# A ring of twelve gather slots instead of thirteen, nine kept weight chunks instead of seven, and a gate computed with tanh

## Time and profile before

| | us |
|---|---|
| median of 3 runs | 1592.19 (1591.38 to 1593.02) |
| the profiled execution | 1590.18 |
| its span | 1588.4 |
| PE busy | 1031.0 (65%) |
| DVE busy | 1108.0 (70%) |
| ACT busy | 465.7 (29%) |
| POOL busy | 569.0 (36%) |
| DMA | 646.25 MB, mean 407 GB/s |

### The profile page before, as it was taken

How to read it: one execution, slowest core, us unless ns; L and a number is a source line. 1 busy time by engine, 2 the same in 40 slices (tenths; PEclk the granted TensorE clock), 3 DMA queues, 4 the chain that set the end, 5 groups by cost and what they waited for, 6 DMA issues and landing times.

```text
span 1588.4 us, 20120 instructions
## 1 busy us (share of the span) xinstructions
PE 1031.0 (65%) x6910; PEld 695.9 (44%) x6910; DVE 1108.0 (70%) x3081; ACT 465.7 (29%) x966; POOL 569.0 (36%) x663
## 2 busy tenths in 40 slices
PE   8996877648634477787674478876676444444444
PEld 8995643426401266665452156655363111111111
DVE  3546878675457776986755776997856777777765
ACT  4111563111101335742211334753222111111112
POOL 0013333333223326742322335762332333333330
PEclk9999876868856698888797679987798555555667
DMA  9999999999999999999999999999999999999995
GB/s 368 409 363 388 380 422 421 418 421 418 417 419 422 421 385 416 414 419 418 421 416 419 422 400 377 421 406 419 421 417 415 423 421 421 422 422 421 421 416 217
DMA packets 105109, 646.25 MB, mean 407 GB/s; under 512 B 11648, under 2 KB 15616, under 8 KB 37424
## 3 DMA queue, kind: packets, MB, share of 16 engines
q0 software_dynamic: 76032, 553.68, 84.3%
q1 hardware_dynamic: 25600, 89.30, 14.2%
q10 hardware_dynamic: 3376, 1.98, 0.4%
HBM read 643.87 MB, written 1.05 MB: 406 GB/s over the span
## 4 chain that ended last, share of the span: by engine, by line
DMA 43%; PE 28%; DVE 15%; issue 4%; ACT 4%; POOL 4%; DVEq 2%; POOLq 0%; ACTq 0%
DMA ring<-in_uv_dram,expert 35%; PE ps L802 14%; PE ps L978 7%; DVE ring L1421 7%; DMA wring<-in_wall_dram 7%; POOL ring L480 4%; PE ps L991 2%; DVE side L1477 1%; PE ps L809 1%; PE ps L1028 1%; ACT side L681 1%; DVE posf L1246 1%; PE ps L966 1%; DVE mix L1438 1%; ACT yg L550 1%
## 5 line engine op out<-in xcount | busy, mean ns | idle before, releaser
L480 POOL DMA_INDIRECT ring<-in_uv_dram,expert x528 | 501.9, 951 | 972.3 <-PE ps L978 636.0
L1421 DVE CUSTOM_DVE_ANT_0 ring<-ring,ps 128x1024 f32<-128x1024 f32 x528 | 634.5, 1218 | 293.3 <-DMA ring<-in_uv_dram,expert 241.5
L978 PE MATMUL ps<-ring,mix 128*32 128x512 f32 x2096 | 362.5, 826 | 322.7 <-DVE mix L1438 322.5
L978 PEld LDWEIGHTS ps<-ring,mix 128*32 128x32 f32 x2096 | 67.2, 135 | 524.3 <-DVE mix L1438 387.6
L640 ACT ACTIVATE gel<-dots 128x4 f32<-128x4 f32 x131 | 26.9, 205 | 747.2 <-DVE dots L1421 746.9
L802 PE MATMUL ps<-yT,wring 128*128 128x128 f32 (+1 forms) x1120 | 148.7, 292 | 48.4 <-DMA wring<-in_wall_dram 32.7
L802 PEld LDWEIGHTS ps<-yT,wring 128*128 128x128 f32 x1120 | 140.4, 200 | 62.7 <-DMA wring<-in_wall_dram 33.2
L991 PE MATMUL ps<-sel,osb 128*128 128x16 f32 x512 | 79.0, 299 | 69.9 <-ACT osb L742 69.9
L991 PEld LDWEIGHTS ps<-sel,osb 128*128 128x128 f32 x512 | 75.7, 234 | 105.5 <-ACT osb L742 105.5
L681 ACT ACTIVATE side<-ident,params 128x128 f32<-128x128 f32 x310 | 96.3, 389 | 14.6 <-PE ps L1028 13.8
L966 PE MATMUL ps<-ident,yg 128*128 128x128 f32 x264 | 48.6, 345 | 64.9 <-DVE dots L1421 64.9
(11 more groups left out here) (270 smaller groups left out, 1205.5 us busy)
## 6 DMA issues: line engine op xcount, KB each, us to landing
wring<-in_wall_dram SPq DMA_DIRECT2D x98, 512.0 KB, 12.7
ring<-in_wall_dram SPq DMA_DIRECT2D x40, 512.0 KB, 15.3
kept<-in_wall_dram SPq DMA_DIRECT2D x28, 512.0 KB, 16.2
ring<-in_uv_dram,expert POOLq DMA_INDIRECT x528, 18.0
osb<-in_wall_dram SPq DMA_DIRECT2D x3, 512.0 KB, 13.0
out_dram<-fo ACTq DMA_DIRECT2D x14, 64.0 KB, 7.0
hT<-in_xT_dram ACTq DMA_DIRECT2D x1, 576.0 KB, 17.2
hT<-in_xT_dram SPq DMA_DIRECT2D x2, 256.0 KB, 3.4
```

The source lines that it names most:

```text
L480: pool.indirect_dma_start(out=ring[:, SLOTS[i], :], out_offset=None, in_=uv, in_offset=bass.IndirectOffsetOnAxis(ap=expert[:, n % 2, k:k + ...
L978: mm = pe.matmul(po[32 * j:32 * j + 32, half, :], mix[:, k, :], ring[:, slot, D + 512 * half:D + 512 * (half + 1)], start=(q == 0), stop=( ...
L1421: nc.vector.tensor_tensor_reduce(out=row, in0=row, in1=yrep, scale=1.0, scalar=0.0, op0=ALU.mult, op1=ALU.add, accum_out=dots[:, k:k + 1]) ...
```

## The change

Three parts:

1. The ring loses a slot: `R` goes from 13 to 12, and `TURN` loses its first entry, 12. The former thirteenth slot was the one that held no weights at the start.
2. `KEEP` goes from 7 to 9: `kept` has two more buffers, which also join the round of early buffers (30 instead of 28 of them).
3. In layer 1 `a * sigmoid(g)` becomes `(tanh(g/2) + 1) * (a/2)`: ACT uses Tanh instead of Sigmoid with `scale=0.5` in both evacuations, POOL halves the bias once at the start (with a semaphore), and DVE uses one `scalar_tensor_tensor` instead of the `tensor_tensor`.

```
-KEEP = 7
-R = 13
+KEEP = 9
+R = 12
...
-    TURN = [12, 4, 5, 6, 7, 0, 1, 2, 3, 8, 9, 10, 11]
+    TURN = [4, 5, 6, 7, 0, 1, 2, 3, 8, 9, 10, 11]
...
+            pool.wait_ge(s_par, 16)
+            pb = params[:, PAR["pw1_b"]:PAR["pw1_b"] + 2 * C]
+            nc.gpsimd.tensor_scalar(pb, pb, 0.5, None, ALU.mult).then_inc(s_hb, 1)
...
+                    if v == 3 and w == 0:
+                        act.wait_ge(s_hb, 1)
...
-                        act.activation(ga[:, c % 4, 0:wi], ps[:, m % 2, 0:wi], ACT.Identity, bias=par("pw1_b", c)
+                        act.activation(ga[:, c % 4, 0:wi], ps[:, m % 2, 0:wi], ACT.Identity, bias=par("pw1_b", c), scale=0.5
...
-                        act.activation(sg[:, c % 4, 0:wi], ps[:, (m + 1) % 2, 0:wi], ACT.Sigmoid, bias=par("pw1_b", C + c)
+                        act.activation(sg[:, c % 4, 0:wi], ps[:, (m + 1) % 2, 0:wi], ACT.Tanh, bias=par("pw1_b", C + c), scale=0.5
...
-                    nc.vector.tensor_tensor(gz[:, c, CK - 1:CK - 1 + wi], ga[:, c % 4, 0:wi], sg[:, c % 4, 0:wi],
-                                            ALU.mult).then_inc(s_gz, 1)
+                    nc.vector.scalar_tensor_tensor(out=gz[:, c, CK - 1:CK - 1 + wi], in0=sg[:, c % 4, 0:wi], scalar=1.0,
+                                                   in1=ga[:, c % 4, 0:wi], op0=ALU.add, op1=ALU.mult).then_inc(s_gz, 1)
```

More of the change, by code:

```diff
@@ L303, in hybrid_trunk @@
         s_pad = sem("s_pad")
+        s_hb = sem("s_hb")
         s_sel = sem("s_sel")
```

## The result

| | before | after |
|---|---|---|
| median of five runs, on one chip | 1592.6 us (1591.38 to 1593.63) | 1599.25 us (1598.74 to 1601.15) |
| ratio | | 1.0047, interval 1.0036 to 1.0058 |
| span of the profiled execution | 1588.4 us | 1597.8 us |
| PE, DVE, ACT, POOL busy | 1031.0, 1108.0, 465.7, 569.0 | 1035.0, 1106.7, 447.7, 570.0 |

The change makes the kernel slower by 0.47%, 6.65 us between the medians. The forecast was slower, by 4.3 us.

What follows compares the result with a forecast made beforehand. The prediction took the kernel to be bound by transfers (1535 of 1588 us). Its terms, -2.5 + 2.5 + 1.6 + 2.7 = +4.3, gave 1596.5 us against the median of 1592.19; 8-in-10 range 1588.0 to 1601.5.

Steps and rivals of the forecast that it cites:

- What bounds: Whole kernel: bound by transfers; late in it a full ring, where one slot less costs nothing.
- Start, -2.5: At the start, two more early buffers let two more chunks load in a DMA hole at 105 to 115 us: -2.5 us.
- Ring in layer 0, +2.5: First half of layer 0: without slot 12 every landing from 131.00 is one gather late, +2.5 us.
- The two dry places: Layer 0, at 131.00 and 186.66: queue dry at both, but the second does not add to the 2.5 us.
- Block 0, +1.6: Layer 1, block 0: three gathers go out after POOL's taps, 3.75 us of delay less 2.1 to spare: +1.6 us.
- the 2.1 us to spare: Block 0: the landing of 9.7 us at 650.85 lies 2.1 us above 7.6, read as a queue just run out.
- Block 1, +2.7: Layer 1, block 1: first gather 1.9 us earlier, then three taps of 4.55 us; second lands at 1061.1, not 1058.4: +2.7 us.
- the gain on PE: Block 1: about half of PE's 5.7 us of chunk waits goes, 3.0, less 1.1 for late landings; releases 1.9 us earlier.
- Tanh, 0: Layer 1's gate: 14 table loads go, 18 us of ACT, but off the path: 0 us.
- four dry points: Gathers landing fast after waits: 131.00 and 186.66 in layer 0, 650.85 and 1050.84 in layer 1's blocks.
- The rival of the fast restart: Thin queue lands a gather in 5.3 us, not 7.6: block 0 loses nothing, block 1 +0.4; 1592.6 us, chance 0.33.
- The rival of the release that comes early enough: PE loses its chunk waits, gather 332 goes before about 1046, shorter ring never felt: -5.0, 1587.2 us, chance 0.21.

Runs made afterwards that it cites:

- short in layer 0: Kernel before, 13 slots in memory, but gathers 0 to 127 wait as with a ring of 12: ratio 1.0021, 3.3 us slower.
- the ring alone: Kernel before with 12 slots instead of 13, still 7 kept chunks and the sigmoid: 1601.59 us, ratio 1.0071.
- the tanh alone: Kernel before with only the gate by tanh, still 13 slots and 7 kept chunks: 1590.31 us, ratio 0.9998.
- the mirror: Kernel before, 13 slots, with POOL's taps behind the second gather of a group, the one that waits there: 1593.37 us, ratio 1.0021.

## Why the prediction was right, and where its sizes were off

The sign and the mechanism stood: slower, because the ring is felt at the dry places, and in the blocks by an order on POOL. One reading of the page was off, the rate: its highest slice is 423 GB/s and not 424, which changes nothing. The rest goes step by step; measured steps are means of the rows of the table.

- **What bounds.** "A ring one slot shorter takes 2.5 us off that and costs nothing there": shown. From group 96 on the lateness of the change is constant to 0.1 us.
- **Start, -2.5.** Between groups 20 and 28 the kernels with nine kept chunks are 1.1 us later than at their own start, those with seven and 12 slots 4.3: -3.2 us. It is not seen at once: up to group 15 both kinds are equally late (3.3 and 3.4 us), and the difference comes with groups 16 and 17. The later gain of block 0's chunks goes the other way first, as the prediction had it ("2.5 us of DMA before the stage"): the lateness of the change goes from 2.7 to 5.2 between groups 28 and 32.
- **Ring in layer 0, +2.5.** Too small. The two kernels with 12 slots and seven kept chunks show 4.3 us by groups 20 to 28 and 3.8 at the end of layer 0. The kernel that only emulates the waits there (short in layer 0) shows 3.2 and 2.7, and costs 3.3 us of time. The two dry places that the prediction read did what it said. Up to group 6 the loss is one gather (2.2 to 2.5 us). At group 7, behind 186.66, the change jumps from 3.6 to 5.9, but by groups 9 and 10 the loss is one gather again (2.4 us above their own start in the mean of the kernels with nine kept chunks, 2.4 in the two with seven, 1.7 in the emulation). What is more than one gather comes later, between groups 11 and 20, of which the prediction had no row. In the ring alone the gathers at 228.61 and 269.22 land in 6.8 and 6.9 us there; that these are the cause is not shown, since the tanh alone has two as fast and loses nothing. So the step that failed is the same as the missed place below: the sum ended with the dry places that had been read.
- **Block 0, +1.6.** The order costs 2.8 us by the traces, as measured with nine kept chunks, because the spare was smaller than read. Landings of 6.0 at 650.35 and 5.3 at 595.65 show that the queue ran empty in block 0, and the 2.1 us to spare above a floor of 7.6 were no measure of that. With 13 slots and the same order the block loses nothing in the mirror's trace, which says that the mechanism needs both, the order and the missing slot. That PE's wait for the last four chunks halves did not happen. PE still gained 1.1 to 2.4 us in this projection in all six kernels with nine kept chunks, and nothing in the two with 12 slots and seven. With the taps moved the block gives back 1.8 us, of the 2.5 of bytes.
- **Block 1, +2.7.** As a sum of two terms one was right and one was not. The order was put at three taps, 4.55 us, and measured 4.4. Of the gain on PE, 1.9 us, little reaches the queue: with the taps out of the way block 1's step is -0.5 and 0.4, and gather 332 goes 0.8 us earlier than the gather it was to beat at 1050.84, once the lateness ahead of the block is taken off (1051.50 less 1.5, and 1054.90 less 4.9). PE itself gains 0.5 to 3.5 us in the projection, too uneven to hang a term on.
- **Tanh, 0**: 0.9998. The Trainium skill (ScalarE: Activation LUTs, section Table sets: the hidden batching unit) leaves tanh out of the set of gelu. This case's trace does not agree: no load stands between the two, and 14 loads are gone. Neither with them nor without them is the time another. DVE's fused instruction was no dearer, 309 ns.
- **The missed place.** The prediction read four dry points. The fifth, at 960 us, was in the page of before (slice 25, 377 GB/s) and in no row that I had taken.
- **The rival of the fast restart** had its fact right: a gather into an empty queue lands in 5.3 to 6.0 us also with a burst behind it (1062.09, followed by 1063.41). It was still no reason for 1592.6. A fast landing says that DMA has run low (123 and 90 GB/s at 1062.09), and that time is the loss. "I read 7.6 as a queue that has just run out" failed in this way: the gather issued at 1050.84 landed 2.5 us after the one ahead of it, one gather's time, so it still stood behind that one.
- **The rival of the release that comes early enough** was refuted twice, by PE's waits (5.4 us as before) and by POOL's, 5.33 us at the gather that it wanted out by 1046 and that went at 1056.65, which is still 1049.4 without the 7.3 us that the trace was late ahead of the block.

By terms: layer 0 +3.4 against +2.5 (ring, start and the chunks moved ahead), block 0 +1.0 against -0.9, block 1 +4.4 against +2.7. That makes 8.8 us in the traces against 4.3; the medians say 6.65 (5.7 to 9.2 by the ratio). All three are off in the same direction, each by its own step: places that had not been read (layer 0, and 960 us), a spare taken from the smallest landing (block 0), and a gain on PE that did not reach the queue (block 1).

## What to carry to other kernels

When the depth of a ring changes, look at which of the issues waits, and keep other work on the issuing engine ahead of that wait and never between it and the rest of the burst: here a change of `k % 4` from 0 to 3 gave back 4.6 of 7.5 us. Look through the whole trace for moments in which a transfer lands near the floor, since those are where depth can have a price. The prices of layer 0 and of the blocks added here (3.3 and 6.5 us against 11.3), while what was lost at 186.66 beyond the first gather was given back. The same memory spent on kept weights gave back 2.5 to 4 us, less than the slot cost.

## What the runs showed of the hardware

- **TensorE at the start.** The same first six chunks take 10.8 us in one execution and up to 12.0 in another, at a granted clock shown as 1.00, the higher of its two levels, 2.4 GHz. Before, then the change:

```profile
4.85 3.47 PE L816 MATMUL ps<-ring,ones 128*128 128x128 f32 x16 [4.85 <-ACT ring L501]
8.16 10.88 PE L802 MATMUL ps<-yT,ring 128*128 128x128 f32 x96
18.97 0.72 PE L831 MATMUL ps<-ring,side 64*128 64x128 f32 x8
```

```profile
4.80 3.75 PE L824 MATMUL ps<-ring,ones 128*128 128x128 f32 x16 [4.80 <-ACT ring L506]
8.35 8.46 PE L810 MATMUL ps<-yT,ring 128*128 128x128 f32 x64
...
20.31 0.71 PE L839 MATMUL ps<-ring,side 64*128 64x128 f32 x8
```

  Behind the sixth chunk stands 18.97 and 20.31; the other kernels lie between 19.09 and 20.42, in no relation to their edits. The first gather inherits it (column start), so a comparison of two single traces has up to 1.6 us of this in it.
- **The clock of one stretch decides a step.** Four kept chunks took 7.39 us at full clock and 9.93 in windows at 0.64 to 0.68, in two executions of one kernel. In the slower one the granted clock was 0.50, the lower level of 1.2 GHz, from 952 to 958 us. In both PE had been idle for 7.1 us, until 938.68 and 937.21, and had worked since with a pause of 1.36 us ahead of 951.98 and 950.76; nothing here says why the clock fell in one and not in the other.
- **A restart is quick.** A gather of 1.05 MB into an empty queue landed in 5.3 to 6.0 us seven times in the change's trace, with further gathers right behind it. The Trainium skill (DMA: Bandwidth & Descriptors, section Anatomy of one DMA) gives 2.0 us plus bytes over 436 GB/s, by which a lone one would land in 4.4 us, an estimate; no run here shows less than 5.3.
